# Fifth and sixth columns in spare PSUM banks, squares added by VectorE in a bank, four weight chunks split ahead of the norm factor

## The chip, the cores and the metric

The kernel runs on one core of a Trainium2 chip. The metric is the device time of one execution in microseconds (us); lower is better. The program works on five engines side by side: TensorE (PE, the matmuls), VectorE (DVE), ScalarE (ACT), GpSimd (POOL) and SyncE (SP, which issues the DMAs). Each engine has its own queue of instructions, run in order; semaphores tie them together.

## The reference

Two layers, each of feed-forward network, mixer, feed-forward network, over 512 positions of width 1024, in float32:

```python
for layer in range(DEPTH):
    g = norm_gains[layer]
    h = rms_norm(x, g[0])
    x = x + 0.5 * rms_norm(swiglu(h, w_ffn_in[layer, 0], w_ffn_out[layer, 0]), g[1])
    h = rms_norm(x, g[2])
    proj = h @ w_in[layer]
    qa, ka, va, qh, fh, ih, gh = jnp.split(proj, splits, axis=-1)
    ya = sliding_window_sink_attention(...)      # 8 heads, window of 128 keys
    yh = hgrn2_mixer(...)                        # gated linear recurrence
    x = x + rms_norm(concat(rms_norm(ya), yh) @ w_out[layer], g[3])
    h = rms_norm(x, g[4])
    x = x + 0.5 * rms_norm(swiglu(h, w_ffn_in[layer, 1], w_ffn_out[layer, 1]), g[5])
```

`rms_norm(x, gain)` is `x * rsqrt(mean(x*x) + eps) * gain`. The factor `rsqrt(...)` is one number per position, so a product with the weights can be made from `x * gain` and multiplied by the factor afterwards.

## The kernel before, in words

**Layout.** `X` holds x transposed: 8 tiles (k = 0 to 7) of 128 features by 512 positions. Every float32 product is made of three matmuls: each operand is split in a high part and a low rest (`HHI`, `HLO` of x times gain; `WHI`, `WLO` of the weights), and high x high, high x low and low x high are added in a PSUM bank. The weights come as a stream of chunks of 128x1024 in four slots: SP loads `RAW`, ScalarE writes `WHI` (`split_hi`, L466, L474), GpSimd writes `WLO` (`split_lo`, L390, L395), TensorE uses both and frees the slot (`w_used`). Freeing of `RAW` (`w_split`) comes from GpSimd.

**PSUM.** Eight banks of 128x512: `bank[0]` to `bank[3]` hold output columns of the products, `bank[4]` to `bank[7]` sums of squares, temporaries and the mixer's scores. A column must have been read by VectorE (`take`, L1083; it multiplies by the norm factor `R` and counts `proj_free`) before the bank is used again (`bank_free`, L766).

**Hand-over.** There are six places where one sublayer ends and the next starts, numbered g = 0 to 5: g = 0, 2, 3 and 5 start a feed-forward network, g = 1 and 4 a mixer. At each, TensorE runs `four` (L795): the first four output columns, k outermost, first all products with `HHI` (`four_high`, L772, started as soon as a part of x is there), then the 32 with `HLO` (`four_low`, L784). Meanwhile VectorE adds the previous result to `X` (L1107, L1159) and writes `HLO` (L1169). ScalarE writes `HHI` (`high`, L487) and the squares of `X` in two slots of `SQ` (`square`, L476), GpSimd adds them in `SS` (`pre`, L398, L415 and L419). TensorE sums `SS` over the partitions with a matmul of ones into `bank[4]` (`total`, L808), which stands after the low products of k = 4 (`TOTAL_AFTER`). ScalarE makes `R` from it (L483, L485), and VectorE's first `take` needs both `R` and the end of its column. Only one weight chunk (c0+4) is split ahead of `R` (L539), the next after it.

**Feed-forward network.** After the four columns a loop of ten rounds makes four columns each, in banks 0 to 3 (L889). VectorE takes two, ScalarE applies Silu, VectorE multiplies, ScalarE writes the high part and VectorE the low part (L1196).

**Mixer.** After `four` come two columns of group 0 (queries of the attention and input of the recurrence, QA and I) in banks 2 and 3, with the transposes of the values (L911) between them. VectorE takes keys, values, F and Q, clears `SM` and `RP`, runs `inputs(0)` (L1231: the gate and tree products of the recurrence, all from SBUF to SBUF), takes QA, runs `keys(0)` (L1241: `KE`), and takes I. ScalarE computes the sigmoids between (`gates`, L637), then splits the next chunks (L655), which GpSimd splits in turn (L431). Then a loop over four pairs of heads follows. Its step t has the attention scores (L970), the transpose of I (L982), a column of the next group, the diagonal scores (L939, recorded at L931, wait for `logit_read` and for `keys(t)`), `scores(0)`, half a column, and then the transposes of the attention's probabilities (L993), which wait for the softmax (`p_ready`) and for VectorE's reading of the diagonal scores (`lv_used`). In later steps `split_lo` waits for VectorE's progress (`staged`, L443, L447, L450, L452).

Of the kernel before, what the change touches and what calls it, by code (L numbers as in the profile page):

```python
# [92 lines left out]
TOTAL_AFTER = 4  # L93
# [30 lines left out]
POOL_TILES = [1, 3, 5, 7]  # L124

# [42 lines left out]
def build_program(nc, xT, stream, params, sinks, rel_bias, one_hot, masks, out):  # L168
    with ExitStack() as ctx:
# [51 lines left out]
        ZHI = sb("ZHI", [P, KT, SEQ], F32R)  # L221
        Slog = S[:, 0:8 * WINDOW].rearrange("p (n k) -> p n k", n=8)
# [6 lines left out]
        bank += [half[:, SEQ * n:SEQ * n + SEQ] for half in pair for n in range(2)]  # L229

# [139 lines left out]
        def _(pool):  # L370
# [27 lines left out]
            def pre(L, s, c0):  # L398

                if L == 0 and s == 0:  # L400
                    for n in range(2):
                        pool.wait_ge(w_hi_first, n + 1)
                        pool.tensor_tensor(WLO[:, n, half_chunk[0]], RAW[:, n, half_chunk[0]], WHI[:, n, half_chunk[0]],
                                           ALU.subtract).then_inc(w_split_first, 1)
                        pool.wait_ge(w_hi, n + 1)
                        pool.tensor_tensor(WLO[:, n, half_chunk[1]], RAW[:, n, half_chunk[1]], WHI[:, n, half_chunk[1]],
                                           ALU.subtract).then_inc(w_split, 1)
                for n in range(2, 4) if L == 0 and s == 0 else range(3):
                    split_lo(L, c0 + n)
                for k in range(1, KT):  # L410
                    if k > 1:
                        pool.drain()
                    pool.wait_ge(sq_done, L * LAYER_SQ + (Q_PRE[s] + k + 1))
                    if k == 1:
                        pool.tensor_tensor(SS[:], SQ[:, 0, :], SQ[:, 1, :], ALU.add).then_inc(sq_free, 2)  # L415
                        if L > 0 or s > 0:
                            split_lo(L, c0 + 3)
                    else:
                        pool.tensor_tensor(SS[:], SS[:], SQ[:, k % 2, :], ALU.add).then_inc(sq_free, 1)  # L419
# [45 lines left out]
        def _(act):  # L465
# [31 lines left out]
            def pre(L, s, c0, cols=CW):  # L497

                g = L * 3 + s
                sq = lambda k: square(L, Q_PRE[s] + k, X[:, k, :])  # L500
                if g == 0:
# [18 lines left out]
                    for k in range(5):  # L520
                        sq(k)
# [15 lines left out]
                for k in range(5, KT):  # L537
                    sq(k)
                split_hi(L, c0 + 4, cols=cols)  # L539
# [65 lines left out]
            def ffn(L, s):  # L605
# [6 lines left out]
                def body(i, first):  # L612
                    for b in range(2):
                        n = (L * 2 + f) * FT + i * 2 + (b + 1)
                        if not first:
                            split_hi(L, c0 + 2 * b + 2, i, 4)
                            split_hi(L, c0 + 2 * b + 3, i, 4)
                        elif b == 0:
                            split_hi(L, c0 + 5)

                        act.wait_ge(proj_free, L * LAYER_JOBS + i * 4 + (j0 + 2 * b + 1 + PROJ_BANKS))
                        act.activation(TMP[:], TMP[:], ACT.Silu).then_inc(silu_ready, 1)  # L622
                        act.wait_ge(u_ready, n)
                        if first and b == 0:
# [3 lines left out]
                body(0, True)  # L628
                with act.Fori(1, FT // 2) as i:
                    body(i, False)  # L630
# [3 lines left out]
            def mixer(L):  # L634
                pre(L, 1, C_KV, CW // 2)
                split_hi(L, C_KV + 5, cols=CW // 2)
# [15 lines left out]
                for c in range(C_GROUP0 + 2, C_GROUPS):  # L652
                    split_hi(L, c, cols=CW // 2)
# [3 lines left out]
                for half in range(2):  # L657
                    act.wait_ge(vwin_full, L * 2 + (half + 1))
                    act.activation(vwin[:, 4 * half:4 * half + 4, :].rearrange("p a b -> p (a b)"), bank[6 + half][:],
                                   ACT.Copy).then_inc(vwin_ready, 1)  # L660
# [84 lines left out]
        def _(pe):  # L745
            def chunk(L, c, tiles, hi, lo, b, i=0, per=0, h_sem=None, h_value=None,
# [8 lines left out]
                for at, k, first, last in tiles:  # L755
                    if h_sem is not None:
                        pe.wait_ge(h_sem, h_value + (k + 1))
# [37 lines left out]
            def four(L, g, c0, order, after_low):  # L795
# [7 lines left out]
                for k in range(KT):  # L803
                    pe.wait_ge(h_lo, g * KT + (k + 1))
                    four_low(c0, k, order)
                    after_low(k)
# [5 lines left out]
            def pre_total(L, s):  # L812

                def at(k):
                    if k == TOTAL_AFTER:
                        total(SS[:], 4, (sq_free, L * LAYER_SQ + (Q_PRE[s] + KT + SQ_SLOTS)), pre_sum)
                return at
# [66 lines left out]
            def ffn(L, s):  # L884
# [3 lines left out]
                four(L, g, c0, (0, 1, 2, 3), pre_total(L, s))  # L888
                with pe.Fori(1, FT // 2) as i:  # L889
# [5 lines left out]
            def mixer(L):  # L895
# [3 lines left out]
                four(L, g, C_KV, (2, 3, 0, 1), pre_total(L, 1))  # L899

                def group0(n):
                    bank_free(L, J_KV + 1 + n, back=1)
                    for part in range(2):
                        ks = FULL[4 * part:4 * part + 4]
                        chunk(L, C_GROUP0 + 2 * n + part, [(k - ks[0][1], k, first, last) for _, k, first, last in ks],
                              HHI, HLO, 2 + n)

                group0(0)
                pe.wait_ge(proj_free, L * LAYER_JOBS + (J_KV + 2 + PROJ_BANKS))
                for n in range(8):  # L910
                    ins = pe.transpose(bank[6 + n // 4][:, (n % 4) * P:(n % 4) * P + P], vT[:, CHUNK * n:CHUNK * n + P], ident[:])  # L911
                    if n % 4 == 3:
                        ins.then_inc(vwin_full, 1)
                group0(1)
# [167 lines left out]
        def _(dve):  # L1082
# [64 lines left out]
            def pre(L, s):  # L1147
# [17 lines left out]
                gain = par[:, L, P_GAIN + 2 * s * KT:]  # L1165
                for k in range(KT):
# [3 lines left out]
                                             in1=HHI[:, k, :], op0=ALU.mult, op1=ALU.subtract).then_inc(h_lo, 1)  # L1170
                    if g == 0 and k == 3:
                        setup_bias()
                if g == 0:
                    setup_bounds()
                dve.wait_ge(pre_r, g + 1)
# [16 lines left out]
            def ffn(L, s):  # L1192
                c0, j0, c1, j1 = ((C_UP0, J_UP0, C_DOWN0, J_DOWN0), None, (C_UP1, J_UP1, C_DOWN1, J_DOWN1))[s]
                pre(L, s)

                def body(i, first):  # L1196
                    for b in range(2):
                        n = (L * 2 + s // 2) * FT + i * 2 + (b + 1)
                        if not (first and b == 0):
                            dve.drain()  # L1200

                        for g, dst in enumerate((TMP, UB)):
                            j = 2 * b + g
                            take(L, c0 + (3 if first else j), dst[:], bank[j][:], i, 4,
# [8 lines left out]
                body(0, True)  # L1213
                with dve.Fori(1, FT // 2) as i:
                    body(i, False)
                down(L, s, c1, j1, DOWN_CHUNKS)

            def mixer(L):
                pre(L, 1)
                dve.memset(kT[:, 0:CHUNK], 0.0)  # L1220
                dve.memset(vT[:, 0:CHUNK], 0.0)
                take(L, C_KV + 3, kT[:, CHUNK:], bank[2][:], four=(1, 0)).then_inc(proj_free, 1)
# [3 lines left out]
                dve.memset(SM[:], 0.0)  # L1226
                dve.memset(RP[:], 0.0)
# [276 lines left out]
```

## Time and profile before

| | us |
|---|---|
| median of 3 runs | 1951.11 (1950.74 to 1951.46) |
| span of the profiled execution | 1950.2 |
| TensorE busy in it | 1921.5 |
| VectorE, ScalarE, GpSimd busy in it | 694.2, 694.0, 870.7 |
| six starts of the low products (`four_low`) at | 24.2, 393.4, 624.6, 991.3, 1358.0, 1589.1 |

The execution that was profiled lasts 0.9 us less by its span than the median of the timed runs, which holds also what lies outside the first and the last instruction. The mean granted clock of TensorE is 0.997 of full speed. In a timeline, a row is a run of equal instructions on one engine; the number in brackets is the time that the engine sat idle before it and what ended that. Ends of matmuls are modelled, so the distance from start to start tells more of a stall than the idle time does.

### The profile page before, as it was taken

To read this page: it belongs to the slowest core of one execution; us is meant where nothing else is said; L and a number is where in the kernel's file an instruction comes from. 1 tells how busy PE (TensorE), PEld (TensorE's weight loads), DVE (VectorE), ACT (ScalarE), POOL (GpSimd) and SP (SyncE) were. 2 spreads that over 40 slices of the span, in tenths; PEclk is the share of its full clock that TensorE was granted. 3 is DMA by queue.
4 is the path that set the end of the run, shared out by engine and by line. 5 is a ranking of instruction groups with operands and counts; after the bars stand their busy time and mean duration, and the time that the engine had idled before them with its cause. 6 is when DMAs were issued, how large, how long until landed. Compare 5 with 4: busy or idle time off the path is not lost.

```text
span 1950.2 us, 29511 instructions
## 1 busy us (share of the span) xinstructions
PE 1921.5 (99%) x11306; PEld 1580.6 (81%) x11306; DVE 694.2 (36%) x1103; ACT 694.0 (36%) x1035; POOL 870.7 (45%) x409
## 2 busy tenths in 40 slices
PE   8999999999999999999999999999999999999997
PEld 6888888877778888888888888888777788888887
DVE  5222210376666322210162222105666672222103
ACT  5323232454545323232353232224554453222221
POOL 6444454453235443444454444455422354434452
PEclk9999999999999999999999999999999999999999
DMA  5332323231212222233222323232321123222231
GB/s 180 106 107 86 107 97 110 95 99 55 67 65 74 101 97 96 97 107 109 88 97 87 107 86 105 100 99 86 108 66 56 61 81 108 97 97 97 98 110 63
DMA packets 54329, 182.82 MB, mean 94 GB/s; under 512 B 6728, under 2 KB 10344, under 8 KB 54248
## 3 DMA queue, kind: packets, MB, share of 16 engines
q1 hardware_dynamic: 54248, 181.65, 27.6%
q8 instruction: 62, 1.02, 0.2%
q14 instruction: 19, 0.16, 0.0%
HBM read 179.14 MB, written 2.49 MB: 93 GB/s over the span
## 4 chain that ended last, share of the span: by engine, by line
PE 92%; DVE 5%; DVEq 1%; ACT 1%; POOLq 0%; issue 0%; DMA 0%; SPq 0%; POOL 0%; ACTq 0%
PE bank L760 26%; PE bank L762 26%; PE bank L761 26%; PE pair L931 2%; DVE HLO L1169 2%; PE bank L789 2%; PE bank L781 2%; PE bank L782 2%; PE pair L760 1%; PE pair L762 1%; PE pair L761 1%; DVE SM L1327 1%; PE pair L810 1%; DVE X L1159 1%; DVE pair L1107 0%
## 5 line engine op out<-in xcount | busy, mean ns | idle before, releaser
L395 POOL TENSOR_TENSOR WLO<-RAW,WHI 128x1024 fp32r<-128x1024 f32 (+1 forms) x334 | 790.4, 2386 | 1016.7 <-ACT WHI L474 847.5
L761 PE MATMUL bank<-HLO,WHI 128*128 128x512 f32 (+1 forms) x1632 | 632.2, 387 | 0.0
L760 PE MATMUL bank<-HHI,WHI 128*128 128x512 f32 x1568 | 620.5, 396 | 1.2 <-DVE TMP L1091 1.0
L762 PE MATMUL bank<-HHI,WLO 128*128 128x512 f32 x1568 | 610.7, 390 | 0.0
L474 ACT ACTIVATE WHI<-RAW 128x1024 fp32r<-128x1024 f32 (+1 forms) x334 | 335.5, 1038 | 82.2 <-PE bank L762 61.6
L761 PEld LDWEIGHTS bank<-HLO,WHI 128*128 128x128 f32 x1632 | 306.6, 188 | 60.4 <-issue 0.5
L760 PEld LDWEIGHTS bank<-HHI,WHI 128*128 128x128 f32 x1568 | 294.2, 188 | 67.2 <-issue 3.2
L762 PEld LDWEIGHTS bank<-HHI,WLO 128*128 128x128 f32 x1568 | 294.3, 188 | 61.9
L760 PE MATMUL bank<-UHI,WHI 128*128 128x512 f32 x616 | 242.7, 394 | 0.0
L762 PE MATMUL bank<-UHI,WLO 128*128 128x512 f32 x616 | 241.5, 392 | 0.0
L761 PE MATMUL bank<-ULO,WHI 128*128 128x512 f32 x616 | 239.0, 388 | 0.0
L627 ACT ACTIVATE UHI<-UB 128x512 f32 (+1 forms) x88 | 55.6, 632 | 467.8 <-DVE UB L1208 467.8
L1091 DVE TENSOR_TENSOR UB<-bank,R 128x512 f32<-128x512 f32 x88 | 60.8, 691 | 372.3 <-PE bank L762 372.3
L1092 DVE COPY Y<-bank 128x512 f32<-128x512 f32 x40 | 27.6, 690 | 386.1 <-PE bank L762 363.6
L762 PEld LDWEIGHTS bank<-UHI,WLO 128*128 128x128 f32 x616 | 115.6, 188 | 27.1
L761 PEld LDWEIGHTS bank<-ULO,WHI 128*128 128x128 f32 x616 | 115.6, 188 | 25.9
L760 PEld LDWEIGHTS bank<-UHI,WHI 128*128 128x128 f32 x616 | 115.8, 188 | 23.0
L559 ACT ACTIVATE SQ<-Y 128x512 f32<-128x512 f32 x40 | 25.3, 632 | 281.2 <-DVE Y L1092 281.2
L1091 DVE TENSOR_TENSOR TMP<-bank,R 128x512 f32<-128x512 f32 x88 | 60.9, 692 | 179.0 <-PE bank L762 168.9
L622 ACT ACTIVATE TMP<-TMP 128x512 f32<-128x512 f32 x88 | 55.6, 631 | 151.9 <-DVE TMP L1091 151.8
L1212 DVE TENSOR_TENSOR ULO<-UB,UHI 128x512 f32 (+1 forms) x88 | 60.9, 692 | 80.2 <-ACT UHI L627 80.2
L781 PE MATMUL bank<-HHI,WHI 128*128 128x256 f32 (+1 forms) x272 | 84.2, 334 | 3.5 <-ACT HHI L494 3.4
(203 smaller groups left out, 1832.5 us busy)
## 6 DMA issues: line engine op xcount, KB each, us to landing
RAW<-stream SPq DMA_DIRECT2D x335, 512.0 KB, 3.7
yT<-X SPq DMA_DIRECT2D x16, 128.0 KB, 1.8
X<-xT SPq DMA_DIRECT2D x3, 512.0 KB, 8.7
RAW<-stream SPq DMA_DIRECT2D x2, 256.0 KB, 3.3
X<-xT SPq DMA_DIRECT2D x2, 256.0 KB, 4.5
bias<-rel_scratch SPq DMA_DIRECT2D x4, 128.0 KB
rel_scratch<-SM SPq DMA_DIRECT2D x1, 382.0 KB
mask_sb<-masks SPq DMA_DIRECT2D x1, 256.0 KB, 8.8
```

The lines of the kernel that those rows point to most:

```text
L395: pool.tensor_tensor(WLO[:, n, 0:cols], RAW[:, n, 0:cols], WHI[:, n, 0:cols], ALU.subtract)\
L474: act.activation(WHI[:, n, 0:cols], RAW[:, n, 0:cols], ACT.Copy).then_inc(w_hi, 1)
L622: act.activation(TMP[:], TMP[:], ACT.Silu).then_inc(silu_ready, 1)
L627: act.activation(u, UB[:], ACT.Copy).then_inc(u_hi, 1)
L760: pe.matmul(dst, WHI[:, slot, lhs], rhs_hi, start=first, stop=False)
L761: pe.matmul(dst, WHI[:, slot, lhs], rhs_lo, start=False, stop=False)
L762: ins = pe.matmul(dst, WLO[:, slot, lhs], rhs_hi, start=False, stop=last)
L781: pe.matmul(bank[j][:, w], WHI[:, slot, lhs], hi[:, k, w], start=start, stop=False)
L782: pe.matmul(bank[j][:, w], WLO[:, slot, lhs], hi[:, k, w], start=False, stop=False)
L789: ins = pe.matmul(bank[j][:], WHI[:, slot, lhs], HLO[:, k, :], start=False, stop=k == KT - 1)
L1091: return dve.tensor_tensor(dst, src, R[:], ALU.mult)
L1212: dve.tensor_tensor(lo, UB[:], hi, ALU.subtract).then_inc(u_lo, 1)
```

## The change

- **Columns 5 and 6.** After `four` (its columns now in the order 2, 3, 0, 1) the next two columns go to banks 5 and 6, which are idle there, and only the third and fourth of that round to banks 2 and 3. So TensorE need not wait for a `take` right behind `four`. In the mixer the two columns of group 0 go to banks 5 and 6, both ahead of the transposes of the values, which go to banks 7 and 2.
- **Squares.** GpSimd adds none any more at a hand-over. ScalarE writes the square of k = 4 into `bank[4]`, the others to `SQ`, `TMP` and `UB`; VectorE adds them one by one in `bank[4]`, between its `HLO` instructions, the last sum to `SS`.
- **The total.** The matmul of ones stands no longer within the low products but in the middle of the fifth column.
- **Weights.** ScalarE splits four chunks (c0+4 to c0+7) ahead of `R`, where it split one.
- **Mixer, VectorE.** The clearing of `SM` and `RP` moves ahead of the wait for `R`; the takes of QA and I move ahead of `inputs(0)` and `keys(0)`. `setup_bounds` moves behind the first network's loop.

```diff
+FIRST_ORDER = (2, 3, 0, 1)
+SECOND_BANKS = (5, 6, 2, 3)
+VWIN_BANKS = (7, 2)
+SUM_BANK, SUM_SQUARE = 4, 4
+SUMS_AFTER = {3: (0, 1), 4: (2,), 5: (3,), 7: (5, 6, 7)}
...
+        PRE_SQ = [SQ[:, 0, :], SQ[:, 1, :], TMP[:], UB[:], None, SQ[:, 0, :], SQ[:, 1, :], TMP[:]]
+        PRE_SQ[SUM_SQUARE] = bank[SUM_BANK]
...
-                for n in range(2, 4) if L == 0 and s == 0 else range(3):
+                for n in range(2, 4) if L == 0 and s == 0 else range(4):
                     split_lo(L, c0 + n)
-                for k in range(1, KT):
-                    ...
-                        pool.tensor_tensor(SS[:], SS[:], SQ[:, k % 2, :], ALU.add).then_inc(sq_free, 1)
...
-                split_hi(L, c0 + 4, cols=cols)
+                for n in range(RAW_SLOTS):
+                    split_hi(L, c0 + 4 + n, cols=cols)
                 act.wait_ge(pre_sum, g + 1)
                 rsqrt_mean(R[:], bank[4][:], D_MODEL).then_inc(pre_r, 1)
...
-                four(L, g, c0, (0, 1, 2, 3), pre_total(L, s))
-                with pe.Fori(1, FT // 2) as i:
+                four(L, g, c0, FIRST_ORDER)
+                for n in range(4):
+                    if n < 2:
+                        pe.wait_ge(x_ready, g * XT)
+                    else:
+                        bank_free(L, j0 + n, 1, 4, back=6)
+                    if n == 0:
+                        chunk(L, c0, FULL[:4], HHI, HLO, SECOND_BANKS[0], 1, 4, done=False)
+                        pre_total(L, s)
+                        chunk(L, c0, FULL[4:], HHI, HLO, SECOND_BANKS[0], 1, 4, ready=False)
+                    else:
+                        chunk(L, c0 + n, FULL, HHI, HLO, SECOND_BANKS[n], 1, 4)
+                with pe.Fori(2, FT // 2) as i:
...
+                four(L, g, C_KV, FIRST_ORDER)
+                pe.wait_ge(x_ready, g * XT)
+                for n in range(2):
                     for part in range(2):
                         ks = FULL[4 * part:4 * part + 4]
                         chunk(L, C_GROUP0 + 2 * n + part, [(k - ks[0][1], k, first, last) for _, k, first, last in ks],
-                              HHI, HLO, 2 + n)
-                group0(0)
+                              HHI, HLO, SECOND_BANKS[n])
+                        if n == 0 and part == 0:
+                            pre_total(L, 1)
...
+                def sum_square(k):
+                    dve.drain()
+                    dve.wait_ge(sq_done, L * LAYER_SQ + (Q_PRE[s] + max(k, SUM_SQUARE) + 1))
+                    last = k == KT - 1
+                    dve.tensor_tensor(SS[:] if last else bank[SUM_BANK], bank[SUM_BANK], PRE_SQ[k], ALU.add).then_inc(sq_free, 2 if last else 1)
...
+                dve.memset(SM[:], 0.0)
+                dve.memset(RP[:], 0.0)
+                dve.wait_ge(pre_r, L * 3 + 2)
                 take(L, C_KV + 3, kT[:, CHUNK:], bank[2][:], four=(1, 0)).then_inc(proj_free, 1)
                 ...
                 take(L, C_KV + 3, PROJ[:, Q, :], bank[1][:]).then_inc(proj_free, 1)
-                dve.memset(SM[:], 0.0)
-                dve.memset(RP[:], 0.0)
+                take(L, C_GROUP0 + 1, PROJ[:, QA, :], bank[SECOND_BANKS[0]][:]).then_inc(proj_free, 1)
+                take(L, C_GROUP0 + 3, PROJ[:, I, :], bank[SECOND_BANKS[1]][:]).then_inc(proj_free, 1)
...
                 inputs(0)
-                take(L, C_GROUP0 + 1, PROJ[:, QA, :], bank[QA][:]).then_inc(proj_free, 1)
                 keys(0)
-                take(L, C_GROUP0 + 3, PROJ[:, I, :], bank[I][:]).then_inc(proj_free, 1)
```

## Rows read from the trace of the kernel before

**Rows 1.** The page's part 1: busy us of each engine (share), instructions.
```profile
PE 1921.5 (99%) x11306; PEld 1580.6 (81%) x11306; DVE 694.2 (36%) x1103; ACT 694.0 (36%) x1035; POOL 870.7 (45%) x409
```

**Rows 2.** TensorE's waits: line, releaser: us in total, times, longest us.
```profile
PE bank L789 <- DVE HLO L1169: 3.3, 3, 1.1
PE pair L810 <- POOL SS L419: 2.0, 1, 2.0
```

**Rows 3.** Timeline of TensorE at g = 3: start, us, instruction, count, [idle before].
```profile
991.34 4.70 PE L789 MATMUL bank<-HLO,WHI 128*128 128x512 f32 x20
995.87 1.02 PE L810 MATMUL pair<-SS,ones 128*128 128x512 f32 x2
996.33 1.50 PE L789 MATMUL bank<-HLO,WHI 128*128 128x512 f32 x4
998.92 2.11 PE L789 MATMUL bank<-HLO,WHI 128*128 128x512 f32 x8 [1.10 <-DVE HLO L1169]
1001.28 0.49 PE L760 MATMUL bank<-HHI,WHI 128*128 128x512 f32 x1 [0.25 <-DVE TMP L1091]
```

**Rows 4.** Timeline of TensorE at g = 0.
```profile
24.20 4.69 PE L789 MATMUL bank<-HLO,WHI 128*128 128x512 f32 x20
30.86 1.73 PE L810 MATMUL pair<-SS,ones 128*128 128x512 f32 x2 [1.97 <-POOL SS L419]
31.61 4.77 PE L789 MATMUL bank<-HLO,WHI 128*128 128x512 f32 x12
36.63 0.49 PE L760 MATMUL bank<-HHI,WHI 128*128 128x512 f32 x1 [0.25 <-DVE TMP L1091]
```

**Rows 5.** A stretch at g = 0: us, busy, PEclk, DMA.
```profile
31.20:36.60 5.40, 5.17 (x14) 3.18 (x12) 0.80 (x2) 3.74 (x5) 2.05 (x2) 0.68 0.67 181
```

**Rows 6.** Timelines of VectorE, then of GpSimd, at g = 3, single instructions.
```profile
990.92 1.77 DVE L1169 SCALAR_TENSOR_TENSOR HLO<-X,par,HHI 128x512 fp32r<-128x512 f32 x1
...
998.79 0.74 DVE L1169 SCALAR_TENSOR_TENSOR HLO<-X,par,HHI 128x512 fp32r<-128x512 f32 x1
...
990.61 1.54 POOL L419 TENSOR_TENSOR SS<-SS,SQ 128x512 f32<-128x512 f32 x1 [0.16 <-issue]
992.30 1.54 POOL L419 TENSOR_TENSOR SS<-SS,SQ 128x512 f32<-128x512 f32 x1 [0.16 <-issue]
```

**Rows 7.** Timeline of TensorE at g = 1.
```profile
393.36 4.70 PE L789 MATMUL bank<-HLO,WHI 128*128 128x512 f32 x20
...
398.61 3.31 PE L789 MATMUL bank<-HLO,WHI 128*128 128x512 f32 x12
...
414.05 1.10 PE L970 MATMUL pair<-kT,PROJ 64*64 64x128 f32 x32
...
421.14 0.69 PE L931 MATMUL pair<-PROJ,KE 64*64 64x64 f32 x32
...
425.55 1.06 PE L993 MATMUL pair<-ident,S 128*128 128x128 f32 x8 [0.29 <-issue]
```

**Rows 8.** Timeline of VectorE at g = 1.
```profile
405.77 0.55 DVE L1234 TENSOR_SCALAR GATE<-GATE,lb_all 128x512 f32<-128x512 f32 x1 [0.40 <-ACT GATE L644]
...
408.54 2.24 DVE L1245 TENSOR_SCALAR KE<-GATE,lb_all 128x512 f32<-128x512 f32 x1
414.16 0.69 DVE L1091 TENSOR_TENSOR PROJ<-bank,R 128x512 f32<-128x512 f32 x1 [3.38 <-PE bank L762]
415.22 1.29 DVE L1281 SCALAR_TENSOR_TENSOR S<-pair,bias 128x512 f32<-128x512 f32 x2 [0.38 <-PE pair L970]
```

**Rows 9.** Timeline of GpSimd, the same stretch.
```profile
408.09 7.28 POOL L395 TENSOR_TENSOR WLO<-RAW,WHI 128x1024 fp32r<-128x1024 f32 x3 [3.08 <-ACT WHI L474]
```

**Rows 10.** Timeline of ScalarE, the same stretch.
```profile
399.21 0.69 ACT L483 ACTIVATE R<-pair,eps 128x512 f32<-128x512 f32 x1 [3.15 <-PE pair L810]
...
405.65 1.28 ACT L645 ACT_TABLE_LOAD   x1
406.95 2.01 ACT L474 ACTIVATE WHI<-RAW 128x1024 fp32r<-128x1024 f32 x2
```

More of the change, by code:

```diff
@@ L519, in pre @@
                     act.activation(lbw[:, 2:4, :], lbw[:, 0:2, :], ACT.Exp).then_inc(setup_act, 1)
-                    for k in range(5):
+                    for k in range(SUM_SQUARE + 1):
                         sq(k)
@@ L610, in ffn, with body @@
                 act.preload_act_table_set("silu_and_others")
[L612 to L615, printed above, removed]
+                def body(i, first=False, split=(0, 1)):
+                    for at in range(2):
+                        b = FIRST_ORDER[2 * at] // 2 if first else at
+                        n = (L * 2 + f) * FT + i * 2 + (at + 1)
+                        if b in split:
                             split_hi(L, c0 + 2 * b + 2, i, 4)
                             split_hi(L, c0 + 2 * b + 3, i, 4)
[L618 to L621 removed]
+                        act.wait_ge(proj_free, L * LAYER_JOBS + i * 4 + (j0 + 2 * at + 1 + PROJ_BANKS))
                         act.activation(TMP[:], TMP[:], ACT.Silu).then_inc(silu_ready, 1)
                         act.wait_ge(u_ready, n)
[L624 removed]
+                        if first and at == 0:
                             act.wait_ge(setup_dma, 80)
@@ L1165, in pre @@
                 gain = par[:, L, P_GAIN + 2 * s * KT:]
+                def sum_square(k):
+                    dve.drain()
+                    dve.wait_ge(sq_done, L * LAYER_SQ + (Q_PRE[s] + max(k, SUM_SQUARE) + 1))
+                    last = k == KT - 1
+                    dve.tensor_tensor(SS[:] if last else bank[SUM_BANK], bank[SUM_BANK], PRE_SQ[k], ALU.add)                        .then_inc(sq_free, 2 if last else 1)
                 for k in range(KT):
@@ L1194, in ffn, with body @@
                 pre(L, s)
[L1196 to L1199, printed above, removed]
+                dve.wait_ge(pre_r, L * 3 + s + 1)
+                def body(i, banks=(0, 1, 2, 3), first=False):
+                    for at in range(2):
+                        b = banks[2 * at] // 2 if first else at
+                        n = (L * 2 + s // 2) * FT + i * 2 + (at + 1)
+                        if not (first and at == 0):
                             dve.drain()
                         for g, dst in enumerate((TMP, UB)):
-                            j = 2 * b + g
-                            take(L, c0 + (3 if first else j), dst[:], bank[j][:], i, 4,
+                            j = 2 * at + g
+                            take(L, c0 + (3 if first else j), dst[:], bank[banks[j]][:], i, 4,
                                  four=(3 * (s // 2), j) if first else None).then_inc(proj_free, 1)
@@ L1212, in body @@
                         dve.tensor_tensor(lo, UB[:], hi, ALU.subtract).then_inc(u_lo, 1)
-                body(0, True)
-                with dve.Fori(1, FT // 2) as i:
-                    body(i, False)
+                body(0, FIRST_ORDER, True)
+                body(1, SECOND_BANKS)
+                with dve.Fori(2, FT // 2) as i:
+                    body(i)
+                if L == 0 and s == 0:
+                    setup_bounds()
                 down(L, s, c1, j1, DOWN_CHUNKS)
```

53 lines of the change are left out of this document (20 added, 33 removed).

## The prediction, made before the change was built

> **What bounds the kernel now.** I read the page's busy times first: TensorE is busy 1921.5 of 1950.2 us, the others under half of that [rows 1]. So only TensorE's stalls can be won, and a stall that is put in anywhere is paid in full. Then its waits: 3.3 us for `HLO` in three places and 2.0 us for GpSimd's sum in one [rows 2]. Those totals are too small, as the ends of matmuls are modelled; so I went to the timelines at the hand-overs and counted from start to start. One matmul of 128x512 takes 0.227 us that way ((4.70 - 0.39)/19 in the twenty that begin at 991.34) [rows 3].
>
> At g = 3 the 32 low products would need 7.25 us; the total among them adds 0.46 us to its own turn and 0.43 us to the four products behind it (1.50 against 1.07 us for four in a row), together 0.9. TensorE should reach the fifth column at 991.34 + 7.25 + 0.9 = 999.5; it starts it at 1001.28 [rows 3]. **Loss 1.8 us**: first for `HLO` of k = 6, then for the take of the first column. g = 2 and g = 5 repeat it (1.10 us of wait each, three in all) [rows 2]. At g = 0 the same sum gives 24.20 + 7.25 + 0.9 = 32.3 against 36.63, a **loss of 4.3 us** [rows 4]. Of this, 1.5 us is the clock: the granted clock averages 0.68 right after the 1.97 us wait, so for about 3.4 us of it TensorE had its lower level of 1.2 GHz [rows 5], and twelve products took 4.77 us where they take 3.31 at full clock [rows 4, 7]. The mixers' starts lose a little ahead of group 0, whose first product waits for the take of the keys.
>
> Why `HLO` is late shows in VectorE's and GpSimd's rows side by side: an `HLO` instruction takes 0.74 us alone and 1.77 us while GpSimd adds squares. The one that begins at 990.92 ends at 992.69, 0.54 us behind the end of GpSimd's addition (990.61 + 1.54 = 992.15); GpSimd's next, issued at 992.30, still takes 1.54 [rows 6]. They exclude one another and go **in turn**. VectorE's takes, which read one operand from PSUM, keep 0.69 us beside GpSimd [rows 8, 9].
>
> **The change part by part, feed-forward networks (g = 0, 2, 3, 5).** GpSimd's seven additions go, VectorE gets seven in a bank. Each has a PSUM operand; the trace has none of that form, so I bound it by the take, 0.69 us [rows 8], and by an addition on GpSimd, 1.54 us [rows 6], and take 0.69 plus 0.1 for the drain, since the take is the same engine with the same kinds of operands. VectorE's queue then is 8 x 0.66 + 7 x 0.78 = 10.7 us, where `HLO` alone took 13. At g = 3, from 986.5 on, `HLO` of k = 3 ends at 989.2, of k = 7 at 994.9, the last sum at 997.2. TensorE wants k = 7 at 991.34 + 28 x 0.227 = 997.7, so the waits for `HLO` go. The total is wanted at 998.6 + 12 x 0.227 = 1001.3: four us of cover. Behind it `R` takes 1.2 us to ScalarE's start (399.21 - 398.05) and 1.4 us for two instructions; the takes of banks 2 and 3 follow at about 1004 and 1004.6, while TensorE is in banks 5 and 6 until 998.6 + 0.9 + 10.9 = 1010.4. **Cover six us**, so the wait for the take goes too. What is late next is the low part of chunk c0+4: ScalarE's seventh square ends at about 992.7, the slot is free at 993.4, so ScalarE ends at 994.5 and GpSimd 2.4 us later at 996.9; wanted at 998.6. At 1.54 us per sum this cover of 1.7 us is just used up. At g = 0 VectorE's first sum waits for the fifth square (about 21.4), and the bias copy behind it is late by 6 us, and with it SP's bias DMAs and the refills queued behind them. Nothing reads those before some 39 us, and the refilled chunk is needed at 54; I cost it at nothing. The total itself moves and is not saved. Sum: **-4.3 - 3 x 1.8 = -9.7 us**. `setup_bounds` moves to where VectorE has a dozen us of idle time: nothing.
>
> **Mixers (g = 1, 4).** TensorE now reaches group 0 at 393.36 + 7.25 = 400.6 [rows 7]. Its 12 products, the total (0.9) and 36 more end at 412.4; the transposes of the values take 0.8, so the scores (L970) start at 413.4, where before it was 414.05. That saves 0.6. But VectorE's queue is another. The take of I waits for the end of the second column, 412.4, and `inputs(0)` and `keys(0)` stand behind it. Before, `inputs(0)` ran at 405.77, while TensorE was in group 0, and the only thing behind I's take (414.16) was the softmax, at 415.22 [rows 8]. Now VectorE sits idle from the take of QA (about 409) to 412.6, and then five SBUF-to-SBUF instructions come ahead of the softmax. Undisturbed they need 2.6 us (0.46 + 0.76 + 0.35 + 0.6 + 0.46 from start to start), so 413.3 + 2.6 = 415.9: **0.7 us late**.
>
> They aren't undisturbed. ScalarE gets the sum at 403.35 + 1.16 = 404.5 (the 1.16 as at 399.21) [rows 10], `R` is there at 405.9, F at 407.9; three sigmoids end at 409.6, the table load of 1.28 at 410.9, and it splits the next chunks from there [rows 10]. GpSimd begins on them 1.1 us later, at **412.05** (408.09 behind 406.95 before), with three in a row, 7.28 us [rows 9, 10]. Before, this met only `KE`: 2.24 us instead of 0.55, ended 0.3 behind GpSimd's first chunk [rows 8]. Now the first of the five (issued 413.3) waits to 414.45. GpSimd's second chunk is queued by then, so in turn: it holds to 417.0, the second instruction ends at 417.5, GpSimd's third chunk holds to 419.8, the other three run freely to 421.1. The softmax starts at 421.05 instead of 415.22: **5.8 us late**. The diagonal scores (wait for `logit_read`) start at 422.4, where TensorE could at 420.6; and L993 waits for VectorE's reading of the diagonal, which stands 10.33 us behind the softmax's start (425.55 - 415.22) [rows 7, 8]: 431.4, while TensorE is there at 426.5. The page shows only 0.29 us of wait at 425.55 [rows 7], but that is because VectorE was just in time; there is no cover. So TensorE is **5.8 us** behind, per mixer, and no later wait in the step is large enough to give it back.
>
> The stall of 4.9 us is longer than the 1.97 us that took the clock down to 1.2 GHz [rows 4, 5]. I add what that cost there, 1.5 us, per mixer; bounds nothing and twice that. Sum: **2 x (5.8 + 1.5) = +14.6 us**.
>
> The Trainium skill (SBUF — State Buffer, section "SBUF: two separate sides") says that VectorE, with two SBUF inputs or in a two-port mode, and GpSimd take a shared port pair for a whole instruction, and the other blocks. The rows agree (1.77 against 0.74 us). It says who has the pair, but not who is next when both wait; by it alone the first of the five waits and the rest could be either this forecast or the second rival.
>
> **Total.** -9.7 + 14.6 = +4.9 us: 1951.1 + 4.9 = **1956.0 us**. The sums are differences within the profiled execution; I add them to the median, which is 0.9 us above its span.
>
> **Rivals.**
> (1) *The collision doesn't happen.* If ScalarE's splits come over 1.3 us later than I count, or VectorE's five instructions earlier, they run beside an idle GpSimd: 0.7 us per mixer. -9.7 + 1.4 = -8.3: 1942.8, faster. It decides at GpSimd's start, 412.05, against VectorE's, 413.3. For it: the times are chained over seven instructions. Against it: GpSimd is busy for 7 us, so a shift of one us only removes one turn.
> (2) *VectorE keeps its turn*, its next instruction being issued ahead of the end of the one before. Then only the drain lets GpSimd in: one chunk less, softmax at 418.8, 3.6 us late, 2.6 us of stall. -9.7 + 2 x (3.6 + 1.5) = +0.5: 1951.6. Against it: with both queued, GpSimd got in at each of seven `HLO` instructions in a row, of which one stands here [rows 6].
> (3) *The sums in the bank are as slow as GpSimd's*, 1.54 us. Then chunk c0+4 is late by up to 1.5 us at four starts: 1956.0 + 6 = 1962. Against it: the takes.
> (4) *The change doesn't do what it says:* `HLO` stays at 1.77 us because of GpSimd's chunk splits. Only one chunk (c0+3) lies near, and ends at 985.6, before the first `HLO`; I leave it at 2 in 100, within (3).
>
> **How the numbers follow.** Forecast 50 in 100, its own range 1953 to 1959 (clock cost nothing to twice). (1) 18; (2) 18; (3) and (4) 9; else 5. The range 1942.5 to 1959.5 takes in the forecast, (2) and most of (1). A measurement of this kernel can tell about 0.2% (3.9 us) from no change. Slower by more than that, over 1955.0: 40 of the forecast's 50, all of (3), 2 of the rest: 0.51. Within: 10 and 17 of (2), 1: 0.28. Faster: (1), 1 of (2), 2 of the rest: 0.21.
>
> **What would show it.** Right: `HLO` at 0.74 us throughout, sums in the bank at 0.69 us, no wait of TensorE at L789 and none behind `four`; in each mixer's first step VectorE's L1234 to L1245 stretched over 7 to 8 us from the take of I, GpSimd's chunks between them, and a wait of near 5 us of TensorE ahead of the transposes of the probabilities, granted clock below 1 behind it. Wrong: GpSimd idle while VectorE runs `inputs(0)`; or sums of over 1 us.

## The result, and the profile after

| | us |
|---|---|
| changed kernel, median of 9 runs | 1956.19 (1955.3 to 1956.5) |
| kernel before beside it, median of 9 runs | 1951.13 (1950.09 to 1952.16) |
| ratio | 1.0024, 95% interval 1.0014 to 1.0033 |
| span of the profiled execution after (before) | 1954.2 (1950.2) |

The change costs 5.1 us in the medians, 4.0 us between the two profiled spans. The engines' busy times (the page's part 1) look as if nothing had happened to TensorE:

```profile
PE 1921.3 (98%) x11306; PEld 1584.6 (81%) x11306; DVE 679.9 (35%) x1145; ACT 694.8 (36%) x1035; POOL 809.7 (41%) x367
```

Its waits (line, releaser, us in total, times, longest) tell more:

```profile
PE pair L1003 <- issue: 9.7, 2, 4.8
PE pair L941 <- DVE SM L1350: 3.3, 6, 0.5
PE pair L941 <- DVE S L1304: 3.2, 2, 1.6
```

The waits for `HLO`, for GpSimd's sum and for the first take [rows 2 to 4] are gone. In their place stand 9.7 us ahead of the transposes of the probabilities (L1003, before it was L993) and 3.2 us ahead of the diagonal scores (L941 for `S`, L1304 is the softmax's first instruction). Both fall twice, once per mixer.

**Where the time went.** The same matmul (the last squares' sum ahead of g = 1, 3, 4 and of the end) and, for g = 2 and 5, the same half-tile of `four_high` were looked up in both traces, start against start:

| from start to | before | after | difference | of which new |
|---|---|---|---|---|
| end of network g = 0 | 377.59 | 372.44 | -5.15 | -5.15 |
| mixer g = 1 done | 616.60 | 618.43 | +1.83 | +6.98 |
| end of g = 2 | 975.55 | 975.44 | -0.11 | -1.94 |
| end of g = 3 | 1342.25 | 1340.26 | -1.99 | -1.88 |
| mixer g = 4 done | 1581.13 | 1587.05 | +5.92 | +7.91 |
| end of g = 5 | 1940.05 | 1944.10 | +4.05 | -1.87 |

Four networks win 10.8 us together and two mixers lose 14.9 us.

**The networks.** TensorE at g = 3, then at g = 0:

```profile
991.25 7.42 PE L794 MATMUL bank<-HLO,WHI 128*128 128x512 f32 x32
998.51 0.39 PE L765 MATMUL pair<-HHI,WHI 128*128 128x512 f32 x1
...
1001.23 1.02 PE L814 MATMUL pair<-SS,ones 128*128 128x512 f32 x2
```

```profile
23.43 7.42 PE L794 MATMUL bank<-HLO,WHI 128*128 128x512 f32 x32
30.69 0.39 PE L765 MATMUL pair<-HHI,WHI 128*128 128x512 f32 x1
```

At g = 3 the 32 low products run in one piece and the fifth column starts at 998.51, 7.26 us after the first of them. In [rows 3] that distance is 9.94 us; of the 2.7 us between them 0.9 is the total, which now stands at 1001.23 in the middle of the fifth column. At g = 0 it is 7.26 instead of 12.43 us [rows 4]; the low products themselves begin 0.77 us earlier there (23.43 against 24.20), by when the first loads landed, which is no doing of the change: in the profiled executions of the edits below, which load in the same way, they begin between 23.35 and 24.40. VectorE at g = 3:

```profile
986.38 2.73 DVE L1187 SCALAR_TENSOR_TENSOR HLO<-X,par,HHI 128x512 fp32r<-128x512 f32 x4
989.21 1.49 DVE L1182 TENSOR_TENSOR pair<-pair,SQ 128x512 f32<-128x512 f32 x2
990.61 0.74 DVE L1187 SCALAR_TENSOR_TENSOR HLO<-X,par,HHI 128x512 fp32r<-128x512 f32 x1
...
993.50 1.41 DVE L1187 SCALAR_TENSOR_TENSOR HLO<-X,par,HHI 128x512 fp32r<-128x512 f32 x2
994.99 1.49 DVE L1182 TENSOR_TENSOR pair<-pair,SQ 128x512 f32<-128x512 f32 x2
996.64 0.69 DVE L1182 TENSOR_TENSOR SS<-pair,TMP 128x512 f32<-128x512 f32 x1 [0.16 <-issue]
```

`HLO` (L1187) takes 0.74 us each (2.73 for four), where it took 1.77 beside GpSimd's additions [rows 6]; a sum in the bank (L1182) takes 0.70 us and 0.79 from start to start. All is done at 997.3, and the total wants it at 1001.2.

**The mixers.** VectorE, then GpSimd, then TensorE at g = 1:

```profile
407.46 0.69 DVE L1101 TENSOR_TENSOR PROJ<-pair,R 128x512 f32<-128x512 f32 x1 [3.71 <-PE pair L767]
408.06 1.31 DVE L1259 TENSOR_SCALAR GATE<-GATE,lb_all 128x512 f32<-128x512 f32 x1
409.30 2.89 DVE L1260 TENSOR_TENSOR PROJ<-PROJ,GATE 128x512 f32<-128x512 f32 x1
412.26 2.47 DVE L1263 TENSOR_TENSOR TREE_F<-GATE 128x256 f32<-128x256 f32 x1
414.65 0.68 DVE L1264 TENSOR_TENSOR QE<-PROJ,GATE 128x512 f32<-128x512 f32 x1
415.25 0.48 DVE L1270 TENSOR_SCALAR KE<-GATE,lb_all 128x512 f32<-128x512 f32 x1
415.65 1.28 DVE L1304 SCALAR_TENSOR_TENSOR S<-pair,bias 128x512 f32<-128x512 f32 x2
```

```profile
406.71 7.73 POOL L401 TENSOR_TENSOR WLO<-RAW,WHI 128x1024 fp32r<-128x1024 f32 x3 [8.99 <-ACT WHI L470]
```

```profile
408.22 1.10 PE L980 MATMUL pair<-kT,PROJ 64*64 64x128 f32 x32
...
416.98 0.69 PE L941 MATMUL pair<-PROJ,KE 64*64 64x64 f32 x32 [1.60 <-DVE S L1304]
...
425.94 1.94 PE L1003 MATMUL pair<-ident,S 128*128 128x128 f32 x8 [4.84 <-issue]
427.81 1.13 PE L941 MATMUL pair<-QE,KE 64*64 64x64 f32 x32
```

VectorE idles 3.71 us ahead of the take of I (L1101), and the five instructions of `inputs(0)` and `keys(0)` behind it take until 415.7. The first waits for GpSimd's first chunk, the second (2.89 us for what took 0.68) for the second, the third (2.47) for the third; the last two run free. The softmax starts 8.2 us behind the take. Before it was 1.06 us [rows 8]. The three chunks take 7.73 us together where they took 7.28 [rows 9]. TensorE waits 1.60 us at 416.98 and 4.84 at 425.94, and behind that the transposes take 1.94 us for eight, at a granted clock (the column behind GpSimd's busy time) of half of full speed, 1.2 GHz:

```profile
425.90:430.40 4.50, 4.46 (x44) 3.75 (x45) 1.88 (x6) 2.14 (x3) 0.34 (x1) 0.50 0.00 0
430.40:434.00 3.60, 3.60 (x73) 2.88 (x72) 2.57 (x4) 0.88 (x2) 2.05 (x1) 0.98 0.12 25
1393.70:1398.40 4.70, 4.64 (x44) 3.93 (x45) 2.08 (x6) 2.14 (x3) 0.53 (x1) 0.50 0.02 3
1398.40:1402.00 3.60, 3.60 (x67) 2.78 (x69) 2.13 (x2) 0.35 (x1) 1.87 (x1) 0.79 0.16 33
```

### The profile page after: what moved, and what is told of

It reads as the page before. It is cut to its first block, busy times and chain, and to the rows that moved or that the text cites. A ratio compares the mean times of both kernels' runs of the same rounds, so it can differ in the third digit from the quotient of the medians.

```text
span 1954.2 us, 29409 instructions
## 1 busy us (share of the span) xinstructions
PE 1921.3 (98%) x11306; PEld 1584.6 (81%) x11306; DVE 679.9 (35%) x1145; ACT 694.8 (36%) x1035; POOL 809.7 (41%) x367
## 3 DMA queue, kind: packets, MB, share of 16 engines
q8 instruction: 65, 1.06, 0.2%
## 4 chain that ended last, share of the span: by engine, by line
PE 94%; DVE 3%; ACT 1%; DVEq 1%; issue 1%; DMA 0%; SPq 0%; POOLq 0%; POOL 0%; ACTq 0%
PE bank L765 25%; PE bank L767 24%; PE bank L766 24%; PE bank L794 3%; PE bank L786 3%; PE bank L787 2%; PE pair L767 2%; PE pair L766 2%; PE pair L765 2%; PE pair L941 2%; DVE SM L1350 1%; PE pair L814 1%; PE pair L1003 0%; PE pair L1049 0%; DMA RAW<-stream 0%
## 5 line engine op out<-in xcount | busy, mean ns | idle before, releaser
L766 PE MATMUL bank<-HLO,WHI 128*128 128x512 f32 (+1 forms) x1536 | 595.5, 388 | 0.0
L765 PE MATMUL bank<-HHI,WHI 128*128 128x512 f32 x1472 | 583.3, 396 | 0.0
L767 PE MATMUL bank<-HHI,WLO 128*128 128x512 f32 x1472 | 574.0, 390 | 0.0
L766 PEld LDWEIGHTS bank<-HLO,WHI 128*128 128x128 f32 x1536 | 289.2, 188 | 57.4 <-issue 0.5
L765 PEld LDWEIGHTS bank<-HHI,WHI 128*128 128x128 f32 x1472 | 276.8, 188 | 59.9 <-issue 0.5
L767 PEld LDWEIGHTS bank<-HHI,WLO 128*128 128x128 f32 x1472 | 276.7, 188 | 58.2
L1101 DVE TENSOR_TENSOR UB<-bank,R 128x512 f32<-128x512 f32 x84 | 58.0, 691 | 360.9 <-PE bank L767 360.9
L1101 DVE TENSOR_TENSOR TMP<-bank,R 128x512 f32<-128x512 f32 x84 | 58.1, 692 | 190.6 <-PE bank L767 164.2
```

Source lines behind the costliest of these rows:

```text
L765: pe.matmul(dst, WHI[:, slot, lhs], rhs_hi, start=first, stop=False)
L766: pe.matmul(dst, WHI[:, slot, lhs], rhs_lo, start=False, stop=False)
L767: ins = pe.matmul(dst, WLO[:, slot, lhs], rhs_hi, start=False, stop=last)
L1101: return dve.tensor_tensor(dst, src, R[:], ALU.mult)
```

## The experiments

All stand against runs of the kernel before on the same chip (median 1951.6 to 1952.0 us there); ratios compare best between runs.

### The take of I behind `inputs(0)` and `keys(0)` again

```diff
-                take(L, C_GROUP0 + 3, PROJ[:, I, :], bank[SECOND_BANKS[1]][:]).then_inc(proj_free, 1)
...
                 inputs(0)
                 keys(0)
+                take(L, C_GROUP0 + 3, PROJ[:, I, :], bank[SECOND_BANKS[1]][:]).then_inc(proj_free, 1)
```

> The changed kernel with one edit: VectorE's take of I moves back behind inputs(0) and keys(0), as it was before the change. Everything else of the change stays. Theory (in turn at the port, behind I's take): inputs(0) starts right behind the take of QA, near 404.3 us, ends near 407 while GpSimd begins at 406.7; the softmax of step 0 starts with the scores, near 409.4 instead of 415.65; the waits of 1.6 and 4.8 us per mixer go, the clock stays at 2.4 GHz; 6.2 us and 1.5 to 2.2 us per mixer are won: 1956.2 - 16 = 1940 us. Rival (the mixers lose by the other columns, banks and transposes, not by VectorE's order): the waits stay, 1954 to 1957 us.

Measured: **1943.79 us**, ratio 0.9958 (0.9944 to 0.9972); faster than both kernels. So the order of VectorE's queue decides and not the columns, banks or transposes. The gain is 12.4 us by the medians (12.9 by the ratios) and not 16, as one wait stayed (TensorE's waits, VectorE's timeline, and the stretch behind the wait):

```profile
PE pair L1003 <- issue: 3.7, 2, 1.8
```

```profile
410.31 1.29 DVE L1304 SCALAR_TENSOR_TENSOR S<-pair,bias 128x512 f32<-128x512 f32 x2 [1.25 <-PE pair L980]
...
413.21 1.74 DVE L1316 SCALAR_TENSOR_TENSOR small<-small,par 128x8 f32<-128x8 f32 x1
```

```profile
422.10:426.00 3.90, 3.81 (x45) 3.17 (x46) 2.48 (x6) 2.03 (x3) 0.90 (x1) 0.70 0.02 4
```

The softmax starts at 410.31, but its fifth instruction (L1304 counts twice), 128x8 numbers, takes 1.74 us: it ends at 414.95, when GpSimd's third chunk does (412.52 + 2.40 = 414.92). TensorE waits 1.8 us, and the clock falls (0.70 of full speed in the 3.9 us behind). This wait was in no sum of mine.

### GpSimd waits, VectorE's late order stays

```diff
                 for c in range(C_GROUP0, C_GROUPS + 3):
+                    if c == C_GROUPS + 1:
+                        pool.wait_ge(staged, L * NT * STAGES + 1)
                     split_lo(L, c, cols=CW // 2 if c < C_GROUPS else CW)
```

> The changed kernel with VectorE's late order left as it is, but GpSimd waits for keys(0) ahead of its second and third full chunk (C_GROUPS+1, +2), as it does in the later steps. Theory (in turn at the port): the first of VectorE's five instructions still waits for GpSimd's first chunk, to about 409.1, the other four run freely and end at 411.6; softmax at 411.6 instead of 415.65, TensorE's wait ahead of the probabilities' transposes 2.5 to 3 us instead of 4.8, none ahead of the diagonal scores; 4.0 us per mixer won: 1948 us if the clock still falls, 1945 if it doesn't. Rival (only the order of the queue counts, the port nothing): 1956 us. Rival (VectorE would have kept its turn): under 2 us per mixer, 1952 or more.

Measured: **1950.97 us**, ratio 0.9996 (0.9986 to 1.0005): 5.5 us below the changed kernel by the ratios (1.0024 - 0.9996 = 0.0028), less than the 8 to 11 expected. VectorE, then GpSimd:

```profile
409.02 1.30 DVE L1261 TENSOR_SCALAR GATE<-GATE,lb_all 128x512 f32<-128x512 f32 x1
410.25 0.68 DVE L1262 TENSOR_TENSOR PROJ<-PROJ,GATE 128x512 f32<-128x512 f32 x1
...
412.44 1.28 DVE L1306 SCALAR_TENSOR_TENSOR S<-pair,bias 128x512 f32<-128x512 f32 x2
...
414.05 1.22 DVE L1316 TENSOR_REDUCE small<-S 128x8 f32<-128x1024 f32 x1
415.34 2.03 DVE L1318 SCALAR_TENSOR_TENSOR small<-small,par 128x8 f32<-128x8 f32 x1
```

```profile
407.67 2.38 POOL L401 TENSOR_TENSOR WLO<-RAW,WHI 128x1024 fp32r<-128x1024 f32 x1 [8.98 <-ACT WHI L472]
412.61 4.74 POOL L401 TENSOR_TENSOR WLO<-RAW,WHI 128x1024 fp32r<-128x1024 f32 x2 [2.56 <-DVE KE L1272]
```

The first part is as the theory has it. Only the first of the five instructions waits (1.30 us, to GpSimd's end at 410.05), the next takes 0.68, and the softmax starts 3.4 us behind the first of them (409.02 to 412.44) instead of 7.6 (408.06 to 415.65). So at least 4.2 us of the mixer's loss is the port's and not the queue's. In the kernel of the experiment above, undisturbed, the same five need 2.65 us (405.31 to 407.96), so the port's whole part in the 7.6 us is near 5.0. But the two chunks that I had held back come at 412.61, and the same small subtraction (L1318 here) waits 1.86 us for the second of them: it ends at 417.37, that chunk at 412.61 + 4.74 = 417.35. Not every instruction in SBUF is stopped: L1316 reduces 128x1024 numbers of `S`, in SBUF, beside these chunks in 1.22 us, the same as in the changed kernel with GpSimd idle. The wait was moved, and I had not asked what the moved chunks meet.

### The stall filled with matmuls, twice

```diff
+                    if t == 0:
+                        pe.wait_ge(vwin_ready, L * 2 + 2)
+                        for n in range(18):
+                            pe.matmul(bank[7][:], WHI[:, (C_GROUPS + 1) % SPLIT_SLOTS, 0:P], HHI[:, 0, :], start=True, stop=True)
                     pe.wait_ge(p_ready, it + 1)
```

> The changed kernel with 18 matmuls of 128x512 more on TensorE in step 0 of each mixer, ahead of the wait for the softmax, into a bank that nobody reads: 4.1 us of work in a wait of 4.8 us. It computes the same. Theory (the stall lowers the clock): the transposes behind it start no later (425.9), the granted clock behind them stays near 1 instead of 0.50, and the 1.5 us (first layer) and 2.2 us (second) that are lost behind them come back: 1956.2 - 3.5 = 1952.7 us. Rival (these microseconds are waits for VectorE's and ScalarE's queues and not the clock): 1956 us or more.

Measured: **1952.90 us**, ratio 1.0005 (0.9995 to 1.0014). The expectation says that it computes the same; it does not: bank 7 holds half of the recurrence's scores of the first level at that point, so these are overwritten. The time is that of the same number and order of instructions. To have it clean, the matmuls went to bank 3, which is free there, and the unedited changed kernel ran beside it:

> The changed kernel itself, unedited, on the chip of the next run, so that small differences are read on one chip: 1.0024 of the kernel before, 1956 us where that takes 1951.

> The changed kernel with 18 matmuls of 128x512 more in step 0 of each mixer ahead of the wait for the softmax, this time into bank 3, which is free there, so that nothing of the result is touched. Theory (the stall's clock): the transposes of the probabilities start no later, the granted clock behind them stays at 1 where it was 0.50, and 1.5 to 2.2 us per mixer come back: 3.5 us less than the changed kernel beside it. Rival (the time behind the stall isn't the clock's): as the changed kernel, within 1 us.

Measured: changed kernel **1956.24 us** (1.0024, 1.0014 to 1.0033), filled **1953.02 us** (1.0008, 0.9999 to 1.0017): 3.2 us less with 8.2 us more work on TensorE. TensorE and the stretch behind the stall, of the filled kernel:

```profile
421.47 4.24 PE L1001 MATMUL bank<-HHI,WHI 128*128 128x512 f32 x18
426.48 1.06 PE L1006 MATMUL pair<-ident,S 128*128 128x128 f32 x8 [0.77 <-issue]
```

```profile
426.00:430.50 4.50, 4.02 (x51) 3.13 (x53) 3.19 (x7) 2.04 (x3) 1.18 (x1) 1.00 0.00 0
```

and of the changed kernel beside it:

```profile
426.44 1.94 PE L1003 MATMUL pair<-ident,S 128*128 128x128 f32 x8 [4.85 <-issue]
```

```profile
426.00:430.50 4.50, 4.06 (x43) 3.45 (x44) 1.95 (x6) 2.14 (x3) 0.00 (x0) 0.50 0.00 0
```

The transposes start at the same time (426.48 and 426.44) but take 1.06 instead of 1.94 us, and the granted clock is 1.00 instead of 0.50. The clock's part of the loss is 3.2 us, 1.6 per mixer on average.

### The squares on GpSimd again

This and the next three start from the kernel with `inputs(0)` ahead of I's take (1943.79 us).

```diff
+                for k in range(1, KT):
+                    if k > 1:
+                        pool.drain()
+                    pool.wait_ge(sq_done, L * LAYER_SQ + (Q_PRE[s] + k + 1))
...
+                        pool.tensor_tensor(SS[:], SS[:], SQ[:, k % 2, :], ALU.add).then_inc(sq_free, 1)
...
-                    for n in SUMS_AFTER.get(k, ()):
-                        sum_square(n)
```

> The same as the kernel with inputs(0) ahead of I's take, but the squares of a hand-over are added by GpSimd again, in SS from two slots of SQ; spare banks, chunks split ahead and place of the total stay. It tells how much of the gain at the feed-forward networks is the squares and how much the banks. If the steps of the sum hold: HLO takes 1.77 us again beside GpSimd's additions, TensorE waits for HLO of k = 6 for 1.1 to 1.3 us at g = 2, 3 and 5, and not for the take; at g = 0 it no longer waits for the total among the low products; so 4 to 5 us slower than that kernel, near 1945. If the banks alone carry the gain: no slower than it, 1940.

Measured: **1967.68 us**, ratio 1.0082 (1.0068 to 1.0095). That is 23.9 us more than the kernel it starts from, where 4 to 5 were expected. (The 1945 of the expectation stands on the 1940 us that I expected of that kernel, not on its 1943.8.) VectorE, GpSimd, TensorE and a stretch at g = 3:

```profile
998.47 2.86 DVE L1192 SCALAR_TENSOR_TENSOR HLO<-X,par,HHI 128x512 fp32r<-128x512 f32 x1
```

```profile
997.95 8.38 POOL L401 TENSOR_TENSOR WLO<-RAW,WHI 128x1024 fp32r<-128x1024 f32 x3
```

```profile
1001.38 1.20 PE L799 MATMUL bank<-HLO,WHI 128*128 128x512 f32 x4 [1.58 <-DVE HLO L1192]
1004.16 2.07 PE L799 MATMUL bank<-HLO,WHI 128*128 128x512 f32 x4 [1.57 <-DVE HLO L1192]
```

```profile
1004.00:1010.00 6.00, 5.84 (x15) 4.59 (x16) 0.10 (x1) 1.06 (x1) 4.69 (x2) 0.54 0.53 178
```

`HLO` of k = 6 and 7 now each wait for a whole weight chunk (2.86 us); TensorE waits 1.6 us for each of the two and runs at 0.54 of its clock behind that. From the first low product to the total 16.7 us pass at g = 3 (993.77 to 1010.45), where it is 10.0 in the changed kernel (991.25 to 1001.23). The same pair of waits stands at g = 2 and g = 5; at g = 0 there is one of 1.7 us for a chunk's low part, at g = 1 and 4 smaller ones. So the parts of the change don't add up one by one: GpSimd's additions cost far more here than they did in the kernel before. My reading is that the four chunks split ahead do it, as they stand ready while `HLO` is still late, where before only one was; no run has GpSimd's additions with one chunk ahead in this kernel, so this is argued from the rows and not shown by itself.

### The networks' columns in banks 0 to 3 again

```diff
-                four(L, g, c0, FIRST_ORDER)
-                for n in range(4):
...
-                with pe.Fori(2, FT // 2) as i:
+                four(L, g, c0, (0, 1, 2, 3))
+                pre_total(L, s)
+                with pe.Fori(1, FT // 2) as i:
```

> The kernel with inputs(0) ahead of I's take, but the feed-forward networks' columns as before: order 0 to 3, the next round in banks 0 to 3 again, the total right behind the low products. Squares on VectorE and four chunks ahead stay. If the spare banks carry what I said (cover for the total, R and the first take): TensorE waits behind each of four low products from the total to the end of the first take, 1.2 + 1.4 + 0.8 = 3.4 us less the total's own 0.5, so 2.9 us at g = 0, 2, 3 and 5, and the clock may fall behind it (1.5 each): 1943.8 + 11.6 = 1955 us, up to 1961. Rival (the squares alone carry the gain): 1944 to 1946.

Measured: **1958.57 us**, ratio 1.0036 (1.0023 to 1.0049), as expected. TensorE and VectorE at g = 3:

```profile
999.64 1.02 PE L814 MATMUL pair<-SS,ones 128*128 128x512 f32 x2
1003.09 0.79 PE L765 MATMUL bank<-HHI,WHI 128*128 128x512 f32 x1 [2.43 <-POOL WLO L401]
```

```profile
1002.26 0.69 DVE L1091 TENSOR_TENSOR TMP<-bank,R 128x512 f32<-128x512 f32 x1 [3.76 <-ACT R L481]
```

From the total to the next column 3.4 us pass, in which `R` is made and the first column taken. The profile names GpSimd's `WLO` as what ended the wait, but the column goes into a bank that the take empties, and the take ends at 1002.26 + 0.69 = 1002.95, just ahead of 1003.09. Without the spare banks the later total is a loss, 14.8 us over four networks. The gap of 3.4 us is there at all four, but the clock fell behind only two of them: at g = 3 the granted clock is 0.50 from 1003.1 to 1006.2 and at g = 2 0.55 over as long, at g = 0 (34.4 to 37.5) and g = 5 it stays at 1.00. Four times 2.9 and two times the 1.5 of the expectation make 14.6.

### One chunk ahead of `R` instead of four

```diff
-                for n in range(RAW_SLOTS):
-                    split_hi(L, c0 + 4 + n, cols=cols)
+                split_hi(L, c0 + 4, cols=cols)
                 act.wait_ge(pre_sum, g + 1)
                 rsqrt_mean(R[:], bank[4][:], D_MODEL).then_inc(pre_r, 1)
+                for n in range(1, RAW_SLOTS):
+                    split_hi(L, c0 + 4 + n, cols=cols)
```

> The kernel with inputs(0) ahead of I's take, but ScalarE splits only one chunk ahead of R and the other three right behind it. R is ready near E + 5.3 (E the end of the low products), the second chunk's high part at E + 6.4, GpSimd's low part at E + 8.8; TensorE wants it at E + 6.4: a wait of 2.4 us at g = 0, 2, 3 and 5, less where the chunk is a half one (mixers: 1.9 us for a half chunk, wanted at E + 3.6: a wait of 3.6), clock cost of up to 1.5 each: 1943.8 + 4 x 2.4 + 2 x 3.6 = 1960 us, up to 1969. Rival (the fourfold split ahead is not needed, R comes early enough): 1944 to 1946.

Measured: **1964.32 us**, ratio 1.0065 (1.0050 to 1.0081), as expected. TensorE waits for the second chunk at all six hand-overs, 2.2 us at each network (2.4 expected) and 3.3 at each mixer (3.6 expected):

```profile
PE pair L766 <- POOL WLO L401: 15.5, 6, 3.3
```

Here too the clock did not fall each time: the granted clock is 1.00 in the 4 us behind the wait of 3.3 us at g = 1 and 0.50 behind the same wait at g = 4.

### The third chunk later

```diff
-                for c in range(C_GROUP0, C_GROUPS + 3):
+                for c in range(C_GROUP0, C_GROUPS + 2):
                     split_lo(L, c, cols=CW // 2 if c < C_GROUPS else CW)
...
                     pool.wait_ge(logit_ready, it + 1)
-                    split_lo(L, C_GROUPS + 4 * t + 3)
+                    split_lo(L, C_GROUPS + 4 * t + (2 if t == 0 else 3))
```

The following three splits of step 0 move one place in the same way.

> The kernel with inputs(0) ahead of I's take, and in step 0 of a mixer GpSimd splits its third full chunk only once the softmax's row maxima are done (logit_ready), the next ones one place later each. In that kernel the third chunk (412.52 to 414.92) held up a subtraction of 128x8 numbers (L1316) for 1.74 us instead of 0.17; TensorE then waited 1.8 us ahead of the probabilities' transposes, and the clock fell again (0.70 and 0.87 in the two stretches of 4 us behind). Theory (a port taken for a whole instruction, whatever the size of the one that waits): L1316 takes 0.17, the wait goes to 0.3 us or less, the clock stays: 1.6 us and about 1.2 us of clock per mixer, 1943.8 - 5.6 = 1938 us. Rival (the chunks moved back now hold up VectorE's later instructions or come late themselves): 1943 or more.

Measured: **1940.37 us**, ratio 0.9941 (0.9927 to 0.9954), the fastest of all. TensorE's wait ahead of the transposes and VectorE's small subtraction:

```profile
PE pair L1005 <- issue: 0.6, 2, 0.3
```

```profile
412.54 0.17 DVE L1318 SCALAR_TENSOR_TENSOR small<-small,par 128x8 f32<-128x8 f32 x1
```

The subtraction takes 0.17 us, the wait is 0.3 us per mixer as before the change [rows 7], and no chunk came late. The gain is 3.4 us; I expected 5.6. A part of the rest is two waits of 0.5 us for `SM` ahead of scores: their total (`DVE SM`) is 4.3 us in eight waits, as before the change, and 3.2 us in six in the kernel that this one starts from.

## Why the prediction was right, point by point

| term | predicted | measured |
|---|---|---|
| network g = 0 | -4.3 | -5.15, of which 0.77 by an earlier first load: -4.4 |
| networks g = 2, 3, 5 | -1.8 each | -1.94, -1.88, -1.87 |
| a sum in the bank | 0.69 + 0.1 | 0.70, 0.79 from start to start |
| `HLO` | 0.74 throughout | 0.74 at g = 2, 3 and 5; beside a half chunk of GpSimd's 1.32 for one at g = 0 and 2.44 for two at g = 1 and 4 |
| softmax's start behind the start of I's take | 8.4 (412.6 to 421.05) | 8.2 (407.46 to 415.65) |
| GpSimd's start ahead of that take | 0.55 (412.05 to 412.6) | 0.75 (406.71 to 407.46) |
| stall at the diagonal, at L993 | 1.8, 4.9 | 1.60, 4.84 |
| mixer up to the transposes | +5.8 | +5.54, +5.71 |
| clock behind the stall, per mixer | +1.5 | +1.44, +2.20 in the trace; 1.6 by the filled stall |
| total | +4.9 | +5.1 (medians), +4.05 (profiled spans) |

The mixer's two last measured terms come from the same rows: the transposes start 0.39 us later than before (425.94 against 425.55) in a trace that was 5.15 ahead at that mixer's start, so 5.54; the rest up to 6.98 comes behind them.

The step that carried the forecast was to ask what VectorE's queue holds behind the take of I. Its proof is the first experiment: the place of one take is worth 12.4 us, port and clock included. That the port adds to it, and in turn, the trace shows by its three stretched instructions, and GpSimd's gating shows it by undoing two of them: 4.2 us of the 5.6 go with them, and with the first one, which stays, the port's part is near 5.0. The sum had 0.7 us for the order alone and 5.1 for the port. Rival (2), VectorE keeping its turn, falls: GpSimd came in after each of the first two instructions, the second of which (L1260) was issued ahead of the end of the first. Rival (1) falls by GpSimd's start, 0.8 us ahead of the take of I; both were on the place predicted after the 5.2 us won at g = 0. Rival (3) falls by the sums' 0.70 us.

The clock's term was taken from a stall of 2.0 us, the nearest row; the stall of 4.8 us cost the same in the first layer and 0.7 more in the second, where the clock came back later (0.79 over the next 3.6 us, where it was 0.98 in the first). That every stall of this length costs its clock was a guess from one row. It held: behind all six such stalls (4.1 to 4.9 us, here, in the changed kernel run again and with GpSimd gated) the granted clock is 0.50 to 0.52. For shorter ones it would not have been safe, as the kernel with one chunk ahead shows (two waits of 3.3 us: 1.00 behind one, 0.50 behind the other).

That the total comes within 0.2 us is partly luck: small misses cancel. The networks won 0.4 us more than the sum had (leaving out the first loads), the mixers lost 0.3 more.

What the prediction did not see, though it didn't touch its number: the port also stops a 128x8 instruction of the softmax. In the changed kernel it starts behind GpSimd's third chunk and is spared; in the first two experiments it met one. I mis-sized three expectations by it or by the same port (the first two experiments and the squares on GpSimd), each time by asking for what a shift removes and not for what it meets.

The Trainium skill (SBUF — State Buffer, section "SBUF: two separate sides") holds here: the pair is taken for a whole instruction (L1316 of the first experiment, two inputs in SBUF: 1.74 us for 128x8 numbers against 0.17), and only by VectorE instructions of the kinds it names. With one of two inputs in PSUM they are not stopped (the sums at 994.99 and 996.64, beside GpSimd's chunks: 0.70 us). That the two engines go in turn when both are queued it does not say; the rows do.

The medians differ by 5.1 us, the two profiled spans by 4.0. That lies in the two executions: where the changed kernel was run again, the median spans are 1954.4 us (10 runs) and 1949.5 us (20 runs of the kernel before), 4.9 apart, and the profiled execution of the kernel before, 1950.2, is a long one among those (1948.7 to 1950.3). What made it longer is open.

## What to carry to other kernels

Before a step is moved ahead in an engine's queue, read what stands behind it: an instruction that waits for another engine's late result holds up everything after it, even what was ready long ago. Where GpSimd and VectorE share the SBUF port, a run of long GpSimd instructions can cost a VectorE instruction that reads two operands from SBUF (or a `TENSOR_SCALAR` from SBUF to SBUF) most of one of them, whatever its size; keep such runs out of VectorE's chains, and add in PSUM what can be added there. And a stall on TensorE may be paid twice, once as wait and once as clock: here all of 4.1 us and more were, and of those between 1.6 and 3.4 us some were and some were not.

## What the runs showed of the hardware that was not expected

A VectorE instruction of 128x8 numbers took 1.74 and 2.03 us instead of 0.17 behind a GpSimd chunk of 2.4 us. The granted clock fell to 0.50 of full speed, 1.2 GHz, behind stalls of 4.8 us and, in part, behind one of 1.8 us (0.70 over 3.9 us); but it stayed at 1.00 behind one of the two waits of 3.3 us in the kernel with one chunk ahead and behind two of the four gaps of 3.4 us in the kernel with the old banks. What sets these apart is open. With the stalls of 4.8 us filled with matmuls of no use it stayed at 1.00, and the kernel was 3.2 us faster with 8.2 us more of TensorE's work.
